# A ring of 20 weight slots in place of 16 in a two-layer encoder trunk, with the expert stage's buffers moved

## The reference, cut to what matters

```
proj = x @ w_in                      # 1024 -> 2208 columns: latent attention, two convolutions, windowed attention
mix  = concat(A, B, C, D) @ w_out    # 1024 x 1024
x    = layer_norm(alpha * x + mix, ln1_g, ln1_b)
aff  = softmax(x @ w_router + b_router)          # 16 experts
gates, idx = top_k(aff.T, 64)                    # every expert chooses 64 tokens
xs   = x[idx]
o    = (silu(xs @ w_gate) * (xs @ w_up)) @ w_down * gates    # three 1024 x 1024 matrices per expert
x    = layer_norm(alpha * x + scatter_add(o, idx), ln2_g, ln2_b)
```

## Time and profile before

| what | us |
|---|---|
| median of 3 runs | 1551.42 (1551.14 to 1551.48) |
| the profiled execution, its own time | 1553.28 |
| its span in the profile | 1551.3 |
| TensorE busy, share of the span | 1378.7, 89% |
| weight queue of SyncE (q1), share of 16 DMA engines | 66.5% |

### The profile page before, as it was taken

How to read it: one execution, slowest core, us unless ns; L and a number is a source line. 1 busy time by engine, 2 the same in 40 slices (tenths; PEclk the granted TensorE clock), 3 DMA queues, 4 the chain that set the end, 5 groups by cost and what they waited for, 6 DMA issues and landing times.

```text
span 1551.3 us, 14745 instructions
## 1 busy us (share of the span) xinstructions
PE 1378.7 (89%) x6044; PEld 683.3 (44%) x6044; DVE 491.4 (32%) x895; ACT 299.6 (19%) x515; POOL 129.1 (8%) x104
## 2 busy tenths in 40 slices
PE   6999899799998988889689998987999988889883
PEld 5666567333333323323277564763333333323331
DVE  5764654401110111100459367443101110101105
ACT  2435540100000000000143536120000000000000
POOL 1330001000000000000253100000000000000003
PEclk9999999799999999999999999989999999999997
DMA  9200332799999999999850012357999999999991
GB/s 383 92 1 1 136 137 82 302 415 428 428 427 428 426 427 428 428 428 429 340 211 0 1 55 96 149 204 288 430 427 426 427 429 426 427 428 428 428 422 62
DMA packets 42482, 462.62 MB, mean 298 GB/s; under 512 B 6704, under 2 KB 7344, under 8 KB 14000
## 3 DMA queue, kind: packets, MB, share of 16 engines
q1 hardware_dynamic: 32544, 434.72, 66.5%
q0 software_dynamic: 4032, 14.68, 2.5%
q10 hardware_dynamic: 5840, 12.29, 2.3%
HBM read 451.18 MB, written 10.49 MB: 298 GB/s over the span
## 4 chain that ended last, share of the span: by engine, by line
PE 62%; DMA 21%; DVE 8%; issue 4%; ACT 2%; POOL 2%; SPq 0%; POOLq 0%; ACTq 0%; DVEq 0%
DMA ring<-w_moe 20%; PE bank L799 18%; PE bank L820 10%; PE bank L482 10%; PE bank L772 7%; PE bank L724 2%; PE bank L728 2%; PE bank L727 2%; PE bank L435 2%; PE bank L544 1%; PE bank L623 1%; DVE X L1281 1%; PE bank L702 1%; DVE X L903 1%; PE bank L514 1%
## 5 line engine op out<-in xcount | busy, mean ns | idle before, releaser
L799 PE MATMUL bank<-ring,work 128*64 128x512 f32 x2048 | 448.7, 594 | 36.2 <-DMA ring<-w_moe 24.4
L799 PEld LDWEIGHTS bank<-ring,work 128*64 128x64 f32 x2048 | 166.4, 137 | 308.3 <-issue 245.2
L820 PE MATMUL bank<-ring,work 128*64 128x512 f32 x1024 | 231.2, 597 | 28.1 <-DMA ring<-w_moe 16.3
L1281 DVE TENSOR_TENSOR X<-X,bank 128x512 f32<-128x512 f32 x128 | 87.9, 687 | 314.2 <-PE bank L772 314.0
L1267 DVE TENSOR_TENSOR work<-work,bank 128x512 f32<-128x512 f32 x32 | 22.0, 688 | 498.6 <-PE bank L799 497.1
L820 PEld LDWEIGHTS bank<-ring,work 128*64 128x64 f32 x1024 | 77.0, 136 | 170.0 <-issue 143.1
L772 PE MATMUL bank<-work 128*128 128x512 f32 x256 | 125.5, 620 | 13.1 <-ACT work L1568 11.2
L1557 ACT ACTIVATE work<-bank 128x512 f32<-128x512 f32 x64 | 38.0, 597 | 358.7 <-PE bank L435 358.7
L482 PE MATMUL bank<-x_hi,w_hi 128*128 128x512 f32 x288 | 79.9, 422 | 6.7 <-ACT x_hi L1332 6.7
L772 PEld LDWEIGHTS bank<-work 128*128 128x128 f32 x256 | 40.7, 188 | 98.5 <-DVE X L1281 45.0
L997 DVE SCALAR_TENSOR_TENSOR bank<-X,par,bank 128x512 f32<-128x512 f32 x120 | 79.9, 750 | 0.9 <-DVE ring L971 0.9
(11 more groups left out here) (184 smaller groups left out, 1369.9 us busy)
## 6 DMA issues: line engine op xcount, KB each, us to landing
ring<-w_moe SPq DMA_DIRECT2D x192, 2048.0 KB, 29.4
ring<-w_in SPq DMA_DIRECT2D x18, 1024.0 KB, 17.2
ring<-w_out SPq DMA_DIRECT2D x8, 1024.0 KB, 23.6
out<-X POOLq DMA_DIRECT2D x12, 512.0 KB, 9.6
X<-out ACTq DMA_DIRECT2D x2, 2048.0 KB, 8.5
x_rows<-X ACTq DMA_DIRECT2D x8, 512.0 KB, 2.6
X<-x_in SPq DMA_DIRECT2D x4, 512.0 KB, 7.5
work<-ln SPq DMA_DIRECT2D x2, 1024.0 KB, 5.1
```

Source lines behind the costliest of these rows:

```text
L799: ins = mm(B((kind, pair, n))[64 * e:64 * e + 64, :], xsT[:, k, 64 * e:64 * e + 64], w[:, e, n * 512:(n + 1) * 512], start=(k == 0), stop= ...
L820: ins = mm(B(("O", pair, n))[64 * e:64 * e + 64, :], hidT[:, k, 64 * e:64 * e + 64], w[:, i, e], start=(k == 0), stop=(k == KD - 1))
L1281: nc.vector.tensor_tensor(X[:, t, cols], X[:, t, cols], B(name)[:, :], ALU.add)\
```

## The change

The ring gets 20 slots. Slots 16 to 19 lie over `work` 0 to 8191. `TURN` has ten entries, so ten pieces can be in the ring. Pieces 3 to 8 (slots 10, 12, 16, 18, 8, 4) now wait for "mix", piece 9 (slot 2) for "logits", and piece n from 10 on for piece n - 10. 96 is not a multiple of ten, so `last_freed` works out which piece used a slot last: 90 to 95 for the first six entries, 86 to 89 for the last four. In the next layer `w` 0 and 1 wait for piece 92, `w` 2 and 3 for piece 89, `w` 4 and 5 for 88, `w` 6 and 7 for 90, `w` 8 for 87; `wout` 2 and 3 wait for 93 and `wout` 1 for 87.

To make room, the expert stage's buffers move: `xs` shrinks to one buffer at `work` 8192, so that the gather of pair p waits for the transposes of pair p - 1; `xsT` lies over `o_sb` at 9216; `hid` lies at 10240; `hidT` lies over `wq` and `wkv`, which become two views of one tensor `w_up`; `G` lies over 512 columns of the constants (`ones`, `rot_a`, `rot_d` and part of `band`). These are loaded again at the start of the second layer by a DMA of ScalarE between `wkv` and `wr`, with the semaphore `consts_back`. TensorE waits for it behind `project(0)` and `project(1)`, VectorE ahead of `d_max(0)`.

`ln2_gb` lies in slot 18 and is loaded by SyncE behind the last piece, when piece 86 has been read. ScalarE's wait and load at line 1551 are gone.

```diff
-TURN = (6, 14, 0, 4, 8, 10, 12, 2)
+N_SLOTS = 20
+TURN = (6, 14, 0, 10, 12, 16, 18, 8, 4, 2)
+LN2_SLOT = 18
...
-    last = PIECES - TURNS + TURN.index(slot - slot % 2)
-    return -1, FREED["chunk", JOINED * last + JOINED - 1]
+    return -1, last_freed(slot)
+
+def last_freed(slot):
+    turn = TURN.index(slot - slot % 2)
+    last = turn + (PIECES - 1 - turn) // TURNS * TURNS
+    return FREED["chunk", JOINED * last + JOINED - 1]
...
+        wq = view(w_up, 0, 2, MLA_H * QK)
+        wkv = view(w_up, 2 * MLA_H * QK, MLA_H * (NOPE + VD))
+        def slots(first, n):
+            if first < RING:
+                return ring[:, first:first + n].rearrange("p a f -> p (a f)")
+            return work[:, (first - RING) * SLOT:(first - RING + n) * SLOT]
...
-        xs = view(work, 4096, 2, D)
-        xsT = view(work, 6144, KD, P)
-        hid = view(work, 7168, FF)
-        hidT = view(work, 8192, KD, P)
+        xs = view(work, 8192, D)
+        xsT = view(work, 9216, KD, P)
         o_sb = view(work, 9216, D)
-        G = view(work, 10240, S)
+        hid = view(work, 10240, FF)
+        hidT = view(w_up, 0, KD, P)
+        G = cst[:, ONES:ONES + S]
-        ln2_gb = view(work, 0, 2 * D)
+        ln2_gb = slots(LN2_SLOT, 1)
...
   (SyncE, behind the loop over the list of loads)
+                sp.wait_ge(freed, at(lay, N_FREED, last_freed(LN2_SLOT)))
+                sp.dma_start(ln2_gb, ln2[lay].partition_broadcast(P)).then_inc(ln2_in, 16)
...
   (TensorE, behind project(0) and project(1))
+                if lay > 0:
+                    pe.wait_ge(consts_back, 16 * lay)
...
-                    pe.wait_ge(xs_full[b], at(lay, 16 * PAIRS // 2, 16 * (pair // 2 + 1)))
+                    pe.wait_ge(xs_full, at(lay, 16 * PAIRS, 16 * (pair + 1)))
...
   (VectorE, ahead of d_max(0))
+                if lay > 0:
+                    hold(consts_back, 16 * lay)
...
   (ScalarE)
+                if lay > 0:
+                    ac.dma_start(cst[:, ONES:ONES + S], consts[:, ONES:ONES + S]).then_inc(consts_back, 16)
                 ac.dma_start(wr[:], w_router[lay].rearrange("(c p) f -> p c f", p=P)).then_inc(params_in, 16)
...
-                ac.wait_ge(xs_full[0], at(lay, 16 * PAIRS // 2, 16))
-                ac.dma_start(ln2_gb, ln2[lay].partition_broadcast(P)).then_inc(ln2_in, 16)
...
   (GpSimd)
-                    if pair >= 2:
-                        hold(fullsem(("xsT", pair - 2, 1)), bank_count(("xsT", pair - 2, 1), lay, 1)[1])
+                    if pair >= 1:
+                        hold(fullsem(("xsT", pair - 1, 1)), bank_count(("xsT", pair - 1, 1), lay, 1)[1])
```

More of the change, by code:

```diff
@@ L75, in ring_loads @@
     order += [("piece", m) for m in range(3, PIECES)]
-    place, count = {}, [0] * RING
+    place, count = {}, [0] * N_SLOTS
     for kind, n in order:
@@ L200, in trunk @@
         par = sb("par", [P, N_PAR])
-        wq = sb("wq", [P, 2, MLA_H * QK])
-        wkv = sb("wkv", [P, MLA_H * (NOPE + VD)])
+        w_up = sb("w_up", [P, 2 * MLA_H * QK + MLA_H * (NOPE + VD)])
         wr = sb("wr", [P, KD, N_EXP])
@@ L265, in trunk @@
         x1T = ring[:, Q_SLOT:Q_SLOT + 2].rearrange("p a f -> p (a f)").rearrange("p (k s) -> p k s", k=KD)
-        xs = view(work, 4096, 2, D)
-        xsT = view(work, 6144, KD, P)
-        hid = view(work, 7168, FF)
-        hidT = view(work, 8192, KD, P)
+        xs = view(work, 8192, D)
+        xsT = view(work, 9216, KD, P)
         o_sb = view(work, 9216, D)
-        G = view(work, 10240, S)
+        hid = view(work, 10240, FF)
+        hidT = view(w_up, 0, KD, P)
+        G = cst[:, ONES:ONES + S]
         aff2 = view(work, 10240, 2, S)
-        ln2_gb = view(work, 0, 2 * D)
-        vals = view(work, 7168, 2, CAP)
-        slotf = view(work, 7168 + 128, 2, CAP)
-        idx = view(work, 7168 + 256, CAP).bitcast(U32)
+        ln2_gb = slots(LN2_SLOT, 1)
+        vals = view(work, 9216, 2, CAP)
+        slotf = view(work, 9216 + 128, 2, CAP)
+        idx = view(work, 9216 + 256, CAP).bitcast(U32)
         trig = view(work, 4096, 6, S)
@@ L291, in trunk @@
         c_rms, c_ln = stat[:, 176:177], stat[:, 177:178]
-        aff = view(work, 7168 + 384, NT, N_EXP)
+        aff = view(work, 9216 + 384, NT, N_EXP)
         banks = [ctx.enter_context(nc.psum_tensor(f"bank{i}", [P, 512], F32)) for i in range(8)]
-        slot_full = [sem(f"slot_full{i}") for i in range(RING)]
+        slot_full = [sem(f"slot_full{i}") for i in range(N_SLOTS)]
         freed = sem("freed")
@@ L326, in trunk @@
         cur_ready = sem("cur_ready")
-        xs_full = [sem(f"xs_full{i}") for i in range(2)]
+        xs_full, consts_back = sem("xs_full"), sem("consts_back")
         g_ready = sem("g_ready")
@@ L413, in _ @@
                             sp.dma_start(ln1_gb, ln1[lay].partition_broadcast(P)).then_inc(ln1_in, 16)
-                        sp.dma_start(ring[:, slot:slot + JOINED].rearrange("p a f -> p (a f)"),
+                        sp.dma_start(slots(slot, JOINED),
                                      w_moe[lay, JOINED * n // PAIR_CHUNKS, n % (PAIR_CHUNKS // JOINED)])\
                             .then_inc(slot_full[slot], 16)
+                sp.wait_ge(freed, at(lay, N_FREED, last_freed(LN2_SLOT)))
+                sp.dma_start(ln2_gb, ln2[lay].partition_broadcast(P)).then_inc(ln2_in, 16)
         def loaded(eng, lay, kind, n):
@@ L775, in _ @@
                 for pair in range(PAIRS):
-                    b = pair % 2
                     def chunk(c):
@@ L783, in chunk @@
                             loaded(pe, lay, "piece", m)
-                        return ring[:, TURN[m % TURNS] + part]
-                    pe.wait_ge(xs_full[b], at(lay, 16 * PAIRS // 2, 16 * (pair // 2 + 1)))
+                        return slots(TURN[m % TURNS] + part, 1)
+                    pe.wait_ge(xs_full, at(lay, 16 * PAIRS, 16 * (pair + 1)))
                     for half in range(2):
-                        transposed(("xsT", pair, half), lay, xs[:, b, half * 512:half * 512 + 512], 4)
+                        transposed(("xsT", pair, half), lay, xs[:, half * 512:half * 512 + 512], 4)
                     for half in range(2):
@@ L1344, in _ @@
                 ac.dma_start(par[:], params[lay]).then_inc(params_in, 16)
-                ac.dma_start(wq[:], w_uq[lay].rearrange("(c p) f -> p c f", p=P)).then_inc(params_in, 16)
-                ac.dma_start(wkv[:], w_ukv[lay]).then_inc(params_in, 16)
+                ac.dma_start(wq, w_uq[lay].rearrange("(c p) f -> p c f", p=P)).then_inc(params_in, 16)
+                ac.dma_start(wkv, w_ukv[lay]).then_inc(params_in, 16)
+                if lay > 0:
+                    ac.dma_start(cst[:, ONES:ONES + S], consts[:, ONES:ONES + S]).then_inc(consts_back, 16)
                 ac.dma_start(wr[:], w_router[lay].rearrange("(c p) f -> p c f", p=P)).then_inc(params_in, 16)
@@ L1633, in gather @@
                     hold(cur_ready, count)
-                    nc.gpsimd.indirect_dma_start(xs[:, b, :], None, x1_rows,
+                    nc.gpsimd.indirect_dma_start(xs, None, x1_rows,
                                                  bass.IndirectOffsetOnAxis(ap=cur[:, b:b + 1], axis=0))\
-                        .then_inc(xs_full[b], 16)
+                        .then_inc(xs_full, 16)
                 for pair in range(PAIRS):
-                    if pair >= 2:
-                        hold(fullsem(("xsT", pair - 2, 1)), bank_count(("xsT", pair - 2, 1), lay, 1)[1])
+                    if pair >= 1:
+                        hold(fullsem(("xsT", pair - 1, 1)), bank_count(("xsT", pair - 1, 1), lay, 1)[1])
                     gather(pair % 2, pair, at(lay, PAIRS, pair + 1))
```

## The result

| | median us | runs | lowest to highest |
|---|---|---|---|
| before | 1551.39 | 4 | 1551.14 to 1551.48 |
| after | 1540.47 | 4 | 1538.72 to 1545.75 |

The ratio is 0.9936 with a 95% interval from 0.9911 to 0.9960: 10.9 us faster, where 13.9 were forecast. The profiled execution of after is the slowest of its four: 1545.75 us, span 1542.8. Run again on another chip, both kernels spread by several us (before 1549.2 to 1556.1 in 11 runs, after 1539.8 to 1544.8 in 6), with the same ratio, 0.9934 (0.9916 to 0.9952). The four close runs of before were no measure of its spread. So the steps are best read stretch by stretch, where the profiles agree much better than the totals.

A forecast was written before the change was run, and what follows sets the result against it. The weight DMA queue, at about 427 GB/s, was taken to set each layer's end. Per layer 9.8 - 2.0 - 1.2 = 6.6, twice 13.2, plus 0.7 gives 13.9: 1537.5 us from the median, 80% range 1533 to 1546.

The forecast's parts named there:

- Two entries: Weight queue's idle hole before each layer's restart: two more pieces load there, gaining 9.8 us per layer.
- The first gather: Start of each expert stage: it meets pieces 8 and 9 still moving and lands later, costing 2.0 us per layer.
- The 2.8 us: Alternative cost of the first gather, standing behind one packet of weights; the sum would then end at 1539.
- The third gather: With one `xs` buffer, pair 2's gather falls into the full weight stream, costing 1.2 us per layer.
- The seam: Between the layers: earlier loads and stores remove TensorE's wait for the first `w_low`, gaining 0.7 us.
- The hole behind the last piece: Layer's end, 754 to 764 us at 106 GB/s: 7.5 us lost before; next loads now follow at once.
- The margin: Second layer's start: reloaded constants land at 795.0, 1 us before TensorE needs them, so cost 0.
- `ln2_gb`, the moved buffers: Layer's end and expert stage: the later load has 8 us of cover, the overlaid buffers add no wait; cost 0.
- TensorE as the bound: Expert stage: TensorE does not become the limit, with 13 us in hand at pair 7.
- a slower stream: Full weight stream: more queued pieces slow it to 416 GB/s, costing 23.2 us, so 1560.7; chance 0.05.
- A wait of some 30 us: Expert stage before: every pair from pair 3 on holds such a wait, ending on a piece of `w_moe`.
- rival (d): Expert stage: restart slips by as much or TensorE bounds, leaving 1550.7 to 1551.4; chance 0.05.

The follow-up runs named there:

- second profile: The changed kernel run again with no edit, on another chip: median 1542.1 us, ratio 0.9934 to the kernel before.
- the gather undisturbed: Changed kernel with piece 9 issued only after the first gather lands: 1535.3 us; with TensorE's wait for the constants also moved to their first use: 1535.1 us.
- longer bridge: Changed kernel with nine instead of five unread TensorE products ahead of the first gather's landing: 1538.2 us, ratio 0.9902 to the kernel before.
- nine entries: Changed kernel with nine entries in the turn, without slots 16 and 17: 1540.2 us, ratio 0.9919 to the kernel before.
- eight entries: Changed kernel with the eight turn entries of before, all else changed, slots 16 and 17 unused: 1557.3 us, ratio 1.0025 to the kernel before.
- later wait: Changed kernel with TensorE's wait for the reloaded constants moved to their first use, three projections later: 1539.7 us, ratio 0.9918 to the kernel before.

## Why the prediction came out as it did

The direction, the main mechanism (two entries fill the hole, and the first gather is charged for it) and the range (1533 to 1546) held. The size was 10.9 us for 13.9, and the sum hid errors of both signs: of the 9.8 us I took off 3.2 per layer, and 5.3 and 4.0 were lost (5.3 and 5.0 in the second profile). That the total is no further off is partly luck, since a third gather that costs nothing makes up for part of a clock that I had not priced. Per layer, step by step:

- **Two entries, +9.8 us: right.** With the gather undisturbed the stages gain 8.6 and 9.9 us in one profile and 10.3 and 9.6 in another, and one entry brings 5.5 and 4.7.
- **The first gather, -2.0: half of it was missing.** It landed 3.1 and 2.3 us later (7.6 and 6.8 against 4.5), and with the clock kept up (longer bridge) the stages lack 2.5 and 2.0 us of the 9.8; so far the step was about right. I priced the late landing as time and did not ask what bridges it: TensorE's unread products end at 305.9 and the gather lands at 309.6. It idled for 3.75 us, its granted clock fell, and transposes, first products and so the restart ran at 1.2 GHz (in the second layer, behind 2.37 us, only the first products). The longer bridge gives that back: 2.9 and 3.0 us. The 2.8 us that the prediction sets beside the 2.0 has no working, and 11.4 against 4.5 us does not show that a gather stands behind one packet of weights and no more: it says only that a full stream makes it 6.9 us longer. The earlier trace rows had shown PEclk at 0.99 from 301 to 311, and the question was what would keep it there. The Trainium skill, "TensorE: Matmul & The Clock Gate", section "Part 1: The HAM clock gate", says that the lower clock is the default and only recent activity of the array lifts it. By that rule an added idle time can cost more than its own length, and this trace agrees (PEclk 0.51 behind 3.75 us).
- **The third gather, -1.2: wrong**, it is 0 within 0.7 us. The restarts say the same: they come 10.9 and 11.0 us behind the gather's issue before, 16.9 and 14.9 in after, 13.9 and 13.1 with the longer bridge, 10.9 and 11.0 with nine entries, and a stage's gain is 9.8 us (4.9 for nine) less that slip, to 0.7 us, with nothing left for the third gather. A stage thus gained 4.5 and 5.8 us (4.5 and 4.8 in the second profile) instead of 6.6.
- **The seam, +0.7: wrong, -0.5.** The hole behind the last piece went, as forecast, and the stores landed at 790.15. But measured from piece 94 that is 3.3 us earlier than before, where I had 5.1, and the constants took 4.1 us for 3.6; so they held TensorE for 1.2 us, in place of the 0.7 for the first `w_low`. The margin I gave it was 1 us.
- **`ln2_gb`, the moved buffers, 0: right.** The end, from piece 94 to the last store, is 39.7 to 39.8 us in all ten profiles.
- **TensorE as the bound, and a slower stream: did not come.** Waits for weights start in pair 5, and the stream runs at 426 and 427 GB/s.
- **"A wait of some 30 us" in every pair from the fourth on: misread.** The 30.14 us of the earlier trace rows are a stretch of the chain that runs through DMAs. What TensorE waits for weights in the whole span of before (us in total, times, longest) is this, some 4 us for each of the ten pairs, and a pair takes 59.95 us instead of 54.55:

```profile
PE bank L799 <- DMA ring<-w_moe: 24.4, 26, 1.3
...
PE bank L820 <- DMA ring<-w_moe: 16.3, 20, 1.3
```

No term of the sum rests on the 30 us. But a pair has 5.4 us of slack and not 30, so they are a weaker argument against rival (d) and for the free moves of buffers than the prediction makes of them.

By the stages and the seam the change is worth 4.5 + 5.8 - 0.5 = 9.8 us in its first profile and 4.5 + 4.8 - 0.4 = 8.9 in the second. That the medians say 10.9 and 10.7 is within the trunk's spread.

## What to carry to other kernels

A deeper prefetch pays for what it moves into a hole of the queue, and is charged where it reaches the small transfer on which the restart hangs. Send the small one first and issue the last large one behind its landing: 6.8 us here for one wait. When a wait gets longer, look at what was keeping TensorE busy during it; a bridge sized to the old wait leaves a gap, and the work behind it can run at the lower clock, as it did here behind 2.37 us and more. And one step's price should be read in its own stretch, since a total that spreads by 5 us can't show it.

## What the hardware showed that I had not expected

A gather of 0.52 MB lands in 4.5 us on an idle queue, in 6.6 to 7.8 when it meets the end of a backlog of weights (in after until about 308, 6 us behind its issue), and in 10.8 to 12.3 in a full stream. Ahead of the first transposes TensorE idled for 2.4 to 3.8 us in five layers of these profiles, and for 4.2 us at the constants in the kernel with eight entries; each time its granted clock was 0.50 to 0.52 soon after. Ahead of the same transposes 1.45 us (later wait, second layer) and anything shorter left it at 1.0, and 1.8 us in the trunk did the one in one execution and the other in another. So did the 2.1 to 2.4 us near 64 us: the clock fell behind them in eight of the ten profiles, behind 2.08 us too, and not behind 2.24 and 2.32 us in after and its second profile. So between 1.8 and 2.4 us the length of one idle time does not decide it; behind the 2.94 us of the routing (near 270 us, and in the second layer) the clock fell in both layers of all ten. The same kernel on one chip stayed within 0.4 us in four runs and spread by 7 and 11 us on two others.
